# A hybrid encoder trunk on one core: only the identity table first, then x, gains and unit 0 in halves, split and multiplied in quarters

## The reference

```python
def rms_norm(x, g):
    y = x * lax.rsqrt(jnp.mean(x * x, axis=-1, keepdims=True) + NORM_EPS)
    return y * g

h = rms_norm(x, ln_mix_e[i])
proj = h @ w_in_e[i]                 # (256, 1024) @ (1024, 1952)
qa, ka, va, q_lat, kv_lat, k_rope = jnp.split(proj, split_e, axis=-1)
```

## Time and profile before

| | |
|---|---|
| median of 3 runs | 1536.21 us (1534.57 to 1536.38) |
| span of the profiled execution | 1535.3 us (no time of its own is given beside the span) |
| TensorE, products | 1475.4 us busy, 96% |
| VectorE | 1136.2 us busy, 74% |
| ScalarE | 959.9 us busy, 63% |
| GpSimd | 79.4 us busy, 5% |
| bytes moved | 425.4 MB, mean 277 GB/s |

### The profile page before, as it was taken

One profiled execution on the slowest core, in us unless ns is written; L12 is line 12 of the kernel. 1 busy time (PEld: TensorE's weight loads), 2 busy tenths in 40 slices (PEclk: granted clock), 3 DMA queues, 4 the chain that ended last, 5 costly groups with the idle time before them and its releaser, 6 DMA issues.

```text
span 1535.3 us, 21503 instructions
## 1 busy us (share of the span) xinstructions
PE 1475.4 (96%) x7978; PEld 1255.1 (82%) x7978; DVE 1136.2 (74%) x825; ACT 959.9 (63%) x863; POOL 79.4 (5%) x80
## 2 busy tenths in 40 slices
PE   6989999999989899999999999999999999999996
PEld 6887999989987688788878878878887887887885
DVE  4474444455374588888888888888888888887886
ACT  5374344345274477767667767767776776776774
POOL 2240000000000000000000000010000000001000
PEclk9999999999999899999999999999999999999999
DMA  9422755555322499999999989989999998998992
GB/s 337 169 83 94 214 191 165 198 183 160 129 83 83 144 367 378 338 329 371 340 324 372 370 305 369 364 332 340 374 342 322 367 359 315 373 375 304 348 366 108
DMA packets 202917, 425.40 MB, mean 277 GB/s; under 512 B 7680, under 2 KB 52992, under 8 KB 202880
## 3 DMA queue, kind: packets, MB, share of 16 engines
q1 hardware_dynamic: 198160, 418.01, 76.2%
q10 hardware_dynamic: 4720, 6.87, 1.6%
HBM read 423.81 MB, written 1.05 MB: 277 GB/s over the span
## 4 chain that ended last, share of the span: by engine, by line
PE 89%; DVE 5%; ACT 3%; issue 2%; DMA 1%; SPq 0%; DVEq 0%; ACTq 0%
PE banks L1106 27%; PE banks L1108 27%; PE banks L1107 27%; PE banks L1366 2%; PE banks L1397 1%; ACT w_hi L409 1%; DVE w_lo L714 1%; PE banks L1264 1%; DMA raw<-in_w_in_e 1%; DVE xn L727 1%; DVE xres L1038 0%; ACT arena L523 0%; DVE qk_lo L1027 0%; PE banks L1162 0%; DVE arena L855 0%
## 5 line engine op out<-in xcount | busy, mean ns | idle before, releaser
L714 DVE TENSOR_TENSOR w_lo<-raw,w_hi 128x2048 fp32r<-128x2048 f32 x397 | 904.1, 2290 | 255.6 <-ACT w_hi L409 255.4
L409 ACT CAST w_hi<-raw 128x2048 fp32r<-128x2048 f32 x397 | 758.6, 1912 | 282.4 <-PE banks L1108 278.4
L1106 PE MATMUL banks<-w_hi,t_hi 128*128 128x512 f32 (+2 forms) x1088 | 418.1, 384 | 5.2 <-DVE w_lo L714 2.7
L1108 PE MATMUL banks<-w_lo,t_hi 128*128 128x512 f32 (+2 forms) x1088 | 411.3, 378 | 0.0
L1107 PE MATMUL banks<-w_hi,t_lo 128*128 128x512 f32 (+2 forms) x1088 | 410.7, 377 | 0.0
L1106 PEld LDWEIGHTS banks<-w_hi,t_hi 128*128 128x128 f32 x1088 | 205.5, 189 | 43.2 <-DVE w_lo L714 4.1
L1108 PEld LDWEIGHTS banks<-w_lo,t_hi 128*128 128x128 f32 x1088 | 205.2, 189 | 38.9
L1107 PEld LDWEIGHTS banks<-w_hi,t_lo 128*128 128x128 f32 x1088 | 205.6, 189 | 36.9 <-issue 0.2
L1106 PE MATMUL banks<-w_hi,h_hi 128*128 128x512 f32 x536 | 209.3, 390 | 0.7 <-DVE w_lo L714 0.7
L1108 PE MATMUL banks<-w_lo,h_hi 128*128 128x512 f32 x536 | 209.2, 390 | 0.0
L1107 PE MATMUL banks<-w_hi,h_lo 128*128 128x512 f32 x536 | 208.7, 389 | 0.0
(11 more groups left out here) (191 smaller groups left out, 1020.6 us busy)
## 6 DMA issues: line engine op xcount, KB each, us to landing
raw<-in_moe_w_gate SPq DMA_DIRECT2D x112, 1024.0 KB, 6.3
raw<-in_moe_w_up SPq DMA_DIRECT2D x112, 1024.0 KB, 6.4
raw<-in_moe_w_down SPq DMA_DIRECT2D x112, 1024.0 KB, 6.6
raw<-in_na_w_qkv SPq DMA_DIRECT2D x12, 1024.0 KB, 5.1
raw<-in_ffn_w_gate SPq DMA_DIRECT2D x11, 1024.0 KB, 5.4
raw<-in_ffn_w_up SPq DMA_DIRECT2D x11, 1024.0 KB, 5.3
raw<-in_ffn_w_down SPq DMA_DIRECT2D x11, 1024.0 KB, 4.9
raw<-in_w_in_e SPq DMA_DIRECT2D x7, 1024.0 KB, 14.9
```

Source lines behind the costliest of these rows:

```text
L409: act.copy(w_hi[:, u.part, 0:n], raw[:, u.raw, 0:n]).then_inc(hi_done, 1)
L714: dve.tensor_tensor(w_lo[:, u.part, 0:n], raw[:, u.raw, 0:n], w_hi[:, u.part, 0:n].bitcast(F32), ALU.subtract).then_inc(lo_done, 1)
L1106: pe.matmul(out, a_hi, b_hi, start=start, stop=False)
L1108: return pe.matmul(out, a_hi, b_lo, start=False, stop=stop)
```

## The change

- **Tables.** ScalarE issues only the 128 columns of the identity at the start (`ident_in`). The other two pieces follow behind the four t_hi casts, ahead of the parameters, both on `tables_in`, so VectorE's rope and GpSimd wait for 32 in place of 16, and so does ScalarE, ahead of the mask cast, which moves behind in_out(0) and stands ahead of in_hi(3).
- **Identity.** Its bf16 cast moves ahead of the warm-up activation of the first norm.
- **Gains** of the first norm move from ScalarE's queue to SP's, behind x.
- **Unit 0** is loaded in two halves (4 k blocks each) with a semaphore each; ScalarE casts it and VectorE subtracts it in four quarters of 512 columns (2 k blocks), VectorE in turn with t_lo; TensorE's new `first_columns` takes k pair by k pair for both token tiles, in banks 4 and 7, so that it waits for one quarter at a time. ScalarE copies q_lat from the two banks by two instructions; unit 3, which uses bank 7, waits for them.
- **Fillers**: eight in place of ten.

```diff
--- before.py
+++ after.py
@@ -258,6 +258,7 @@
         gain_in = [sem(f"gain_in{i}") for i in range(5)]
         lat_in, router_in, rpb_in = sem("lat_in"), sem("router_in"), sem("rpb_in")
         tab_b = sem("tab_b")
+        ident_in, w0_full, w0_hi, w0_lo = sem("ident_in"), sem("w0_full"), sem("w0_hi"), sem("w0_lo")
         ss_done, ms_done = sem("ss_done"), sem("ms_done")
         std_done, rstd_done, xn_ready = sem("std_done"), sem("rstd_done"), sem("xn_ready")
         t_mm, t_hi_done, t_lo_done = sem("t_mm"), sem("t_hi_done"), sem("t_lo_done")
@@ -335,7 +336,11 @@
 
             for t in range(T):
                 sp.dma_start(xres[:, t, :], x[0, t * P:(t + 1) * P, :]).then_inc(x_in[t], 16)
-            for i, (c0, n) in enumerate(IN_COLS):
+            sp.dma_start(gains[:, 0, :], over_partitions(ln_mix_e, D)).then_inc(gain_in[0], 16)
+            for half, full in enumerate((w0_full, raw_full[0])):
+                dst = raw[:, 0, half * UNIT // 2:(half + 1) * UNIT // 2].rearrange("p (k n) -> p k n", k=KD // 2)
+                sp.dma_start(dst, w_in[:, 4 * half:4 * half + 4, 3 * A_W:3 * A_W + QL]).then_inc(full, 16)
+            for i, (c0, n) in list(enumerate(IN_COLS))[1:]:
                 load(Unit(U_IN + i), w_in[:, :, c0:c0 + n])
             for i in range(4):
                 load(Unit(U_OUT0 + i), w_out[:, 2 * i:2 * i + 2, :])
@@ -397,8 +402,7 @@
 
         @block.scalar
         def _(act):
-            act.dma_start(gains[:, 0, :], over_partitions(ln_mix_e, D)).then_inc(gain_in[0], 16)
-            act.dma_start(tab[:], tables).then_inc(tables_in, 16)
+            act.dma_start(tab[:, C_ID:C_ID + P], tables[:, C_ID:C_ID + P]).then_inc(ident_in, 16)
 
             def hi(u, n=UNIT):
 
@@ -413,6 +417,9 @@
                 act.activation(warm_out.pop(), one, func)
 
             def norm_stats(n, after=None):
+                if n == 0:
+                    act.wait_ge(ident_in, 16)
+                    act.copy(ident_b[:], ident).then_inc(tab_b, 1)
 
                 warm(ACT.Sqrt)
                 for t in range(T):
@@ -436,11 +443,15 @@
 
             act.wait_ge(tab_b, 1)
             norm_stats(0)
-            act.wait_ge(tables_in, 16)
-            act.copy(ident_b[:], ident).then_inc(tab_b, 1)
-            act.copy(mask_b[:], tab[:, C_MASK:C_MASK + GRID_W]).then_inc(tab_b, 1)
-            hi(Unit(0))
+
+            for i in range(4):
+                if i % 2 == 0:
+                    act.wait_ge((w0_full, raw_full[0])[i // 2], 16)
+                cut = slice(i * UNIT // 4, (i + 1) * UNIT // 4)
+                act.copy(w_hi[:, 0, cut], raw[:, 0, cut]).then_inc(w0_hi if i < 3 else hi_done, 1)
             split_t_hi(0)
+            act.dma_start(tab[:, 0:C_ID], tables[:, 0:C_ID]).then_inc(tables_in, 16)
+            act.dma_start(tab[:, C_TRI:C_ALL], tables[:, C_TRI:C_ALL]).then_inc(tables_in, 16)
             act.dma_start(lat_gain[:, 0:QL], over_partitions(mla_q_norm, QL)).then_inc(lat_in, 16)
             act.dma_start(lat_gain[:, QL:QL + KVL], over_partitions(mla_kv_norm, KVL)).then_inc(lat_in, 16)
             act.dma_start(uq[:], mla_w_uq[0].rearrange("(k p) n -> p k n", p=P)).then_inc(lat_in, 16)
@@ -465,6 +476,10 @@
 
                 act.wait_ge(used, U_IN + i + 1)
                 src = banks[:, 4 + i % 4, :].rearrange("p (a b) -> p a b", a=2)[:, :, 0:IN_COLS[i][1]]
+                if i == 0:
+                    act.copy(ql[:, 0, :], banks[:, 4, 0:QL])
+                    act.copy(ql[:, 1, :], banks[:, 7, 0:QL]).then_inc(proj_out, 1)
+                    return
                 last = queries(qa_t[0], i - 2, src) if i in (2, 3) else act.copy(in_dst[i], src)
                 last.then_inc(proj_out, 1)
 
@@ -474,6 +489,8 @@
             in_hi(1)
             in_hi(2)
             in_out(0)
+            act.wait_ge(tables_in, 32)
+            act.copy(mask_b[:], tab[:, C_MASK:C_MASK + GRID_W]).then_inc(tab_b, 1)
             in_hi(3)
             in_out(1)
 
@@ -736,8 +753,14 @@
                                       t_hi[:, 2 * i:2 * i + 2, :].bitcast(F32), ALU.subtract).then_inc(t_lo_done, 1)
 
             norm_apply(0, 0)
-            lo(Unit(0))
-            split_t_lo(0)
+            for i in range(4):
+                dve.wait_ge(w0_hi if i < 3 else hi_done, i + 1 if i < 3 else 1)
+                cut = slice(i * UNIT // 4, (i + 1) * UNIT // 4)
+                dve.tensor_tensor(w_lo[:, 0, cut], raw[:, 0, cut], w_hi[:, 0, cut].bitcast(F32),
+                                  ALU.subtract).then_inc(w0_lo if i < 3 else lo_done, 1)
+                dve.wait_ge(t_hi_done, i + 1)
+                dve.tensor_tensor(t_lo[:, 2 * i:2 * i + 2, :], banks[:, i, :].rearrange("p (k s) -> p k s", k=2),
+                                  t_hi[:, 2 * i:2 * i + 2, :].bitcast(F32), ALU.subtract).then_inc(t_lo_done, 1)
 
             def in_lo(i):
                 lo(Unit(i), 8 * IN_COLS[i][1])
@@ -785,7 +808,7 @@
 
             cos = tab[:, C_COS:C_COS + 32].rearrange("p (t c) -> p t c", t=T)
             sin = tab[:, C_SIN:C_SIN + 32].rearrange("p (t c) -> p t c", t=T)
-            dve.wait_ge(tables_in, 16)
+            dve.wait_ge(tables_in, 32)
 
             def rope(x1, x2, c, s, tmp, y1, y2, step):
 
@@ -1162,20 +1185,36 @@
                     pe.matmul(banks[:, bank, :].rearrange("p (r c) -> p r c", r=4), ident_b[:],
                               ident_b[:].unsqueeze(1).broadcast_to([P, 4, P]), start=True, stop=True)
 
-            pe.wait_ge(tables_in, 16)
+            pe.wait_ge(ident_in, 16)
             pe.wait_ge(tab_b, 2)
-            keep_busy(7, 10)
+            keep_busy(7, 8)
             transpose_xn(0)
 
+            def first_columns():
+
+                hi_w, lo_w = unit_parts(Unit(0), KD, QL)
+                for k in range(KD):
+                    if k % 2 == 0:
+                        pe.wait_ge(w0_lo if k < 6 else lo_done, k // 2 + 1 if k < 6 else 1)
+                        pe.wait_ge(t_lo_done, k // 2 + 1)
+                    for m in range(2):
+                        cut = slice(m * P, (m + 1) * P)
+                        last = three(banks[:, 4 + 3 * m, 0:QL], t_hi[:, k, cut], t_lo[:, k, cut],
+                                     hi_w[:, k, :], lo_w[:, k, :], k == 0, k == KD - 1)
+                last.then_inc(used, 1)
+
 
             def in_proj(i):
+                if i == 3:
+                    pe.wait_ge(proj_out, 1)
                 if i >= 4:
                     pe.wait_ge(proj_out, i - 3)
                     if i >= 6:
                         pe.wait_ge(qk_rest, i - 5)
-                columns(Unit(i), 4 + i % 4, IN_COLS[i][1], 2 <= i < 6, 0 if i == 0 else None).then_inc(used, 1)
-
-            for i in range(4):
+                columns(Unit(i), 4 + i % 4, IN_COLS[i][1], 2 <= i < 6).then_inc(used, 1)
+
+            first_columns()
+            for i in range(1, 4):
                 in_proj(i)
             pe.wait_ge(lat_v, 3)
             for k in range(2):
@@ -1490,7 +1529,7 @@
             last.then_inc(lat_zero, 1)
             pool.wait_ge(lat_zero, 1)
 
-            pool.wait_ge(tables_in, 16)
+            pool.wait_ge(tables_in, 32)
             for h in range(AH):
                 if h == 1:
                     pool.wait_ge(lat_p, 3)
```

## The result

The changed kernel takes 1548.51 us, median of 5 runs (1546.56 to 1548.72), against 1536.21 us (5 runs of the kernel before, 1532.67 to 1536.38). The ratio is 1.0083 with a 95% interval of 1.0071 to 1.0096: **12.3 us slower**, where 2.8 us faster was forecast, and outside the range. The profiled execution took 1548.72 us, with a span of 1546.9 (before 1535.3), so its rows carry 11.6 of the 12.3.

What follows compares the result with a forecast made beforehand. TensorE was taken as the bound, with 89% of the chain. Unit 1's start moves from 23.83 to 21.0, after 2.0 lost to the low clock: 1536.2 - 2.8 = 1533.4 us, range 1531.4 to 1536.6.

Steps and rivals of the forecast that it cites:

- Part 1: Landing order at the start: unit 0's halves land at 9.3 and 10.7, unit 1 at 12.5.
- Part 2: First norm on ScalarE: identity lands 4.8, cast 0.28, then one table load; Squares 6.6 and 8.2, second xn 11.3.
- the table load costs double: Rival, first norm: a second 1.28 on ScalarE puts the first product at 14.45, leaving 1.5 gained, 1534.7 us; chance 0.07.
- Part 3: Unit 0 in quarters: first product at 13.15 instead of 18.00, unit 0 would end at 19.0.
- Part 4: ScalarE's DMA issues before unit 1's cast: nine from 12.4 end at 17.0, unit 1 ready at 19.8; gain 4.0.
- Part 5: Mask cast, second ql copy and waits for bank and tables cost nothing; only the tables' worst landing costs some 2.5 us.
- Part 6: Unit 0's first products run at 1.2 GHz, losing 2.0 us; unit 0 ends at 21.0, gain 2.8.
- backed-up rival: ScalarE's issues before unit 1's cast stall, starting it 7.1 later; unit 1 ready at 26.9, 1539.3 us; chance 0.08.
- high clock: Rival, unit 0: fillers lift the clock and transposes hold it; 4.0 gained, 1532.2 us; chance 0.25.

Runs made afterwards that it cites:

- mended kernel: Changed kernel with router and last gains issued behind unit 3's cast, Sqrt warm-up ahead of the identity wait: 1530.09 us, ratio 0.9966; repeated on another chip 1530.73, 0.9971.
- long router rows: Changed kernel with the router loaded as 128 rows of 256 B instead of 1024 of 32 B (routing differs): 1532.33 us in one run.
- gains later: Changed kernel with the last gains' issue moved from ahead of unit 1's cast to behind the casts of units 1 and 2: 1534.35 us, ratio 0.9991.
- filled gap: Changed kernel with 37 filler products on TensorE between unit 0 and unit 1, stall left in: 1543.10 us, ratio 1.0059.
- tables alone: Kernel before with only the change's table part (identity first, other pieces ahead of the parameters, mask cast moved), unit 0 whole, ten fillers: 1551.30 us, ratio 1.0101.
- late triangle: Changed kernel with the second table piece (triangle and constants, 128 rows) issued behind unit 3's cast: 1534.33 us, ratio 1.0002.
- fillers in the gaps: The mended kernel with one more filler behind tile 0's transposes and three behind tile 1's: 1529.11 us, ratio 0.9962.

## Why the prediction was wrong

**Part 1, landings: right.** The identity landed at 4.7 (4.8 forecast), and neither half of unit 0 made a quarter wait.

**Part 2, the identity and the table load: the smaller miss.** I put the cast ahead of the load and costed it at 0.28. The trace shows load, cast, load. The Squares start at 7.80 and 9.26, not 6.6 and 8.2, and the fillers at 6.52. This is the rival "the table load costs double", which had 0.07. My evidence against it, that no cast in the earlier trace rows shows a load, was weak: in the kernel before every cast came after the Sqrt load, so those rows could not show what a cast does as the first instruction. The Trainium skill (ScalarE: Activation LUTs, Table sets) has copy in every table set, so that a cast alone never needs a change of set. The trace agrees as far as all later casts go; but when none was loaded yet the cast brought one, 1.28 us, and the Sqrt behind it another, 1.28 us. The mended kernel shows the price and the remedy: with the warm-up ahead of the wait there is one load, and the Squares start at 4.87 and 6.34.

**Part 3, quarters: right in mechanism.** The first product came at 14.91, where the double load's own figure was 14.45; with the level high throughout it came at 14.70 in the kernel with long router rows. That the mended kernel's 13.20 meets the 13.15 of the forecast is luck. Its Squares ran 1.7 earlier than forecast, and other waits took that back: VectorE waited 0.91 for the gains, ScalarE 0.39 for the second half of unit 0, and the casts to t_hi stood behind the quarters.

**Part 4 is the step that failed.** "Each takes 0.51 ... nine from 12.4 end at 17.0." Eight did (0.34 to 0.49); the ninth took 7.96, and unit 1 was ready at 29.4 instead of 19.8. Of these 9.6, 7.5 are the stall and 2.3 the later start of the nine, at 14.74, behind the double load of part 2 (the other issues and the casts were 0.2 quicker than forecast). I had named the rival, priced the stall at 7.1 in all (7.5 beyond the usual length was measured), and given it 0.08, since "none of the seven passed 0.59". That row says nothing about an eighth and a ninth: 1920 rows fit, 2176 don't. The count was in the code. A sign may have been in the earlier trace rows, where SP's issues of weights, 1024 rows each, last 2.88 in the median; I had read those as SP's own habit and never counted rows on either queue. No run shows that they have the same cause.

**Part 5, costed at nothing: right.** The tables were there by 22.5, the mask cast ran at 30.08, and TensorE waited for none of it.

**Part 6, the clock: right kind, wrong place.** I gave 2.0 us to the first products. They lost 0.5: the level was low from 14.91 to 16.1. "Here the level has first to rise" was wrong as well. In the kernel before, eight of the ten fillers start 0.43 apart, the last two 0.22. In the changed kernel the level rose within the fillers too: the transposes of tile 0 are 0.11 apart, those of tile 1 0.21 apart again, so it fell in the idle time between them. But what I had priced there, that TensorE comes back from an idle stretch at 1.2 GHz, cost 6.6 in units 1 and 2, and no case of mine had it. The backed-up rival stopped at 1539.3 because it added the wait of unit 1 and not what follows a wait. With its own stall and the 6.6 it would have said 1545.9. **So the step that failed is a stall that had the wrong chance, and behind it a term is missing that makes half of the loss.**

**The whole.** With the stall moved and nothing else, unit 1 starts 2.4 and 3.2 earlier than in the kernel before (21.44, 20.66), but the runs show no gain: ratios 0.9991 and 1.0002. The forecast 2.8 were not confirmed by any kernel that has the two table loads. The mended kernel gains 4.1, and that this is near the 4.0 of the high clock is luck too, since it owes part of it to the earlier warm-up, which the forecast did not contain. The change as written gives all of this away, and more, through 128 rows too many in one queue.

What stays open: which event frees the room, and so what exactly is counted. In the changed kernel, the one with the gains later, the filled gap and the tables alone, the stalled issue ended within 0.15 us of the landing of uq, at 26.55, 28.05, 27.30 and 28.76, but the late triangle's ended 1.6 after it. It is not simply the rows that have not landed yet. In the mended kernel four of the issues, 512 rows, had landed by 21.0, and still the last gains waited from 22.63 to 25.11, up to the landing of uq at 25.0. Nor does SP's queue stop at the same sum. In the changed kernel 2432 rows had gone out on it with the issue of unit 1, before any had landed, and only the next issue waited:

```profile
3.45 0.59 SPq L335 DMA_DIRECT2D raw<-in_w_in_e  x1
4.08 3.69 SPq L335 DMA_DIRECT2D raw<-in_w_in_e  x1
```

So "more than 2048 and at most 2176" holds for the rows of this batch on ScalarE's queue, and is no limit to carry to another queue.

## What to carry to other kernels

Count the rows (contiguous runs) that go out on an engine's queue in one batch before adding to it, above all those of narrow matrices, and put the issues that nobody needs soon behind the next cast that TensorE waits for. Price a wait of TensorE's as long as those here (3.89 and 7.96 us) as the wait plus the products behind it at half the clock, and fill it if it can't be avoided; the mended kernel's wait of 1.41 cost nothing beyond itself. Put the warm-up activation ahead of any other instruction of ScalarE, a plain cast included.

## What the runs showed of the hardware that I had not expected

**An issue can block the engine that makes it.** The issue took 7.96, 9.41, 9.38 and 8.41 us, and nothing behind it on ScalarE ran, against 0.34 to 0.60 up to 2048 rows. The DMA share stood at 1.06 during the stall of the changed kernel. Full DMA engines alone do not do it: with the long router rows the share was 1.11 from 14.0 to 18.2, and no issue in that time took over 0.49.

**A dense stream of 160-column products ran at the low level from end to end.** 48 products of 160 columns, without a gap, stayed at 0.50 for 10.3 us, and the level rose 3.8 us into the 256-column ones. At that level a product of 160 columns takes 0.213, as long as one of 256 columns. The Trainium skill (TensorE: Matmul & The Clock Gate, Part 1) has the level set by how busy TensorE was recently; the trace has it busy for 10.57 of 10.60 us here and the level did not rise, so this stretch does not bear that out.

**The level differs from one profile to the next where the code is the same.** Up to the first product of unit 0 the changed kernel and four of its variants compute with the same instructions. The first product was at 1.2 GHz in the profiles of the changed kernel and of the one with the gains later, and at 2.4 in those of the long router rows, the filled gap and the late triangle. And from the router's first product to the first product of the experts seven of the twelve profiles show 16.8 us, four 13.5 and that with fillers in the gaps 18.4; the mended kernel's own two profiles have 13.5 and 16.8. The windows of that stretch, changed kernel first, then the late triangle's:

```profile
504.80:521.60 16.80, 16.77 (x91) 12.65 (x92) 6.96 (x30) 7.33 (x11) 1.52 (x4) 0.70 0.01 1
```

```profile
490.30:503.90 13.60, 13.51 (x93) 10.87 (x93) 6.96 (x30) 7.43 (x11) 1.56 (x5) 0.87 0.01 2
```

The granted clock differs (0.70 against 0.87), the work does not. These 3.3 us are as much as the runs of one kernel scatter here. They may be why the kernels that mend only the stall, 2.3 and 2.8 us ahead at the router's stage, are not separable from the kernel before by their medians; that was not followed up.
